# The last up unit of each feed-forward by halves of tokens

## The reference

```python
def swiglu(h, w_gu, w_down):
    gu = h @ w_gu
    g, u = jnp.split(gu, 2, axis=-1)
    return (jax.nn.silu(g) * u) @ w_down
```

## Time and profile before

| | |
|---|---|
| median of three runs | 2002.74 us (2000.58 to 2003.66) |
| span of the profiled execution | 1994.7 us |
| what lies around the span, against the median | 8.0 us |
| TensorE busy | 1939.8 us, 97% |
| VectorE busy | 1178.0 us, 59% |
| ScalarE busy | 977.8 us, 49% |

### The profile page before, as it was taken

One profiled execution on the slowest core, in us unless ns is written; L12 is line 12 of the kernel. 1 busy time (PEld: TensorE's weight loads), 2 busy tenths in 40 slices (PEclk: granted clock), 3 DMA queues, 4 the chain that ended last, 5 costly groups with the idle time before them and its releaser, 6 DMA issues.

```text
span 1994.7 us, 23044 instructions
## 1 busy us (share of the span) xinstructions
PE 1939.8 (97%) x8950; PEld 1559.6 (78%) x8950; DVE 1178.0 (59%) x1544; ACT 977.8 (49%) x1522; POOL 202.7 (10%) x273
## 2 busy tenths in 40 slices
PE   5999999999999999999999999999999999999998
PEld 4768768888888888668788888887777778888886
DVE  6777699899999999663443333335445453333323
ACT  4533268888888888553243222124455542222221
POOL 3200211131211110020010000001011110000001
PEclk9999999999999999999999999999999999999999
DMA  8564589999999999942322323223212142323201
GB/s 297 173 214 170 180 295 364 369 376 374 374 372 371 358 369 362 350 128 81 106 82 89 104 85 105 95 74 105 67 43 85 43 136 86 106 86 105 95 32 42
DMA packets 200024, 366.49 MB, mean 184 GB/s; under 512 B 13514, under 2 KB 84055, under 8 KB 199914
## 3 DMA queue, kind: packets, MB, share of 16 engines
q1 hardware_dynamic: 181152, 343.20, 49.1%
q10 hardware_dynamic: 8714, 11.17, 1.6%
q0 software_dynamic: 10048, 10.62, 1.6%
HBM read 365.05 MB, written 24.65 MB: 195 GB/s over the span
## 4 chain that ended last, share of the span: by engine, by line
PE 83%; DVE 7%; DMA 4%; ACT 2%; issue 2%; POOL 1%; ACTq 0%; POOLq 0%; DVEq 0%
PE ps L288 80%; DVE wlo L235 3%; DMA raw<-in_w_expert_gate 3%; ACT whi L216 1%; PE ps L2215 1%; DMA VR<-in_b_subln 1%; PE ps L2242 1%; DVE XT0l L2298 0%; PE ps L2907 0%; ACT YB L2307 0%; ACT whi L220 0%; DVE acc L285 0%; PE ps L790 0%; DVE hT4l L856 0%; DMA raw<-in_ada_w 0%
## 5 line engine op out<-in xcount | busy, mean ns | idle before, releaser
L235 DVE TENSOR_TENSOR wlo<-raw,whi 128x1024 fp32r<-128x1024 f32 x574 | 671.1, 1214 | 295.0 <-ACT whi L216 292.3
L216 ACT ACTIVATE whi<-raw 128x1024 fp32r<-128x1024 f32 x574 | 571.5, 1048 | 214.2 <-PE ps L288 191.1
L288 PE MATMUL ps<-hT5h,whi 128*128 128x512 f32 x352 | 137.0, 389 | 0.6 <-DVE hT5l L285 0.6
L288 PE MATMUL ps<-hT3h,whi 128*128 128x512 f32 x352 | 137.0, 389 | 0.6 <-DVE hT3l L285 0.6
L288 PE MATMUL ps<-hT5l,whi 128*128 128x512 f32 x352 | 136.9, 389 | 0.0
L288 PE MATMUL ps<-hT3h,wlo 128*128 128x512 f32 x352 | 136.9, 389 | 0.0
L288 PE MATMUL ps<-hT5h,wlo 128*128 128x512 f32 x352 | 136.9, 389 | 0.0
L288 PE MATMUL ps<-hT3l,whi 128*128 128x512 f32 x352 | 136.9, 389 | 0.0
L2770 DVE TENSOR_TENSOR tmpT<-tmpT,ps 128x512 f32<-128x512 f32 x44 | 30.1, 684 | 139.3 <-PE ps L288 139.3
L288 PE MATMUL ps<-whi,XT1h 128*128 128x512 f32 x256 | 102.7, 401 | 1.5 <-DVE XT1l L2298 1.5
L288 PE MATMUL ps<-whi,XT0h 128*128 128x512 f32 x256 | 102.7, 401 | 1.1 <-DVE XT0l L2298 1.1
(11 more groups left out here) (475 smaller groups left out, 4102.4 us busy)
## 6 DMA issues: line engine op xcount, KB each, us to landing
raw<-in_w_expert_gate SPq DMA_DIRECT2D x64, 1024.0 KB
raw<-in_w_expert_up SPq DMA_DIRECT2D x64, 1024.0 KB
raw<-in_w_expert_down SPq DMA_DIRECT2D x64, 1024.0 KB
raw<-in_ffn_w_gu SPq DMA_DIRECT2D x44, 1024.0 KB
raw<-in_ffn_w_down SPq DMA_DIRECT2D x20, 1024.0 KB
raw<-in_ada_w SPq DMA_DIRECT2D x24, 512.0 KB, 5.0
raw<-in_a_w_in SPq DMA_DIRECT2D x8, 1024.0 KB
raw<-in_kv_w SPq DMA_DIRECT2D x8, 1024.0 KB
```

Source lines behind the costliest of these rows:

```text
L216: e.activation(hi[:, c], raw[:, c], ACT.Copy).then_inc(self.S("w_hi"), 1)
L235: e.tensor_tensor(lo[:, c], raw[:, c], hi[:, c].bitcast(F32), ALU.subtract).then_inc(self.S("w_lo"), 1)
L288: return e.matmul(o, l, r, start=start, stop=stop, skip_group_check=True)
```

## The change

The last u unit of each feed-forward (`ng == 10`) is made by a new function. It goes through the tokens by halves: 256 moving columns into a bank of its own for each half and block, so four banks and 96 products in place of two banks and 48. VectorE multiplies and ScalarE and VectorE split the rows by the same halves. The low parts of this unit are so counted four times, and `a_lo` goes to 24 per feed-forward. The first half of the last down product waits at `tb == 0` for the rows of the first half of tokens and at `tb == 2` for those of the second half. Some semaphores are put together (`mix_lo` and `gm_lo` as `left_lo`, `mix_hi` and `gm_hi` as `left_hi`, `fga` and `fgb` as `final_in`), with the later waits moved on by the earlier counts.

```diff
-                    R.plan(f"fu{l}.{ng}", 2, V_)
-                    W.ends[W.index[f"fu{l}"][ng]] = R.full(f"fu{l}.{ng}", 1)
+                    R.plan(f"fu{l}.{ng}", 4 if ng == 10 else 2, V_)
+                    W.ends[W.index[f"fu{l}"][ng]] = R.full(f"fu{l}.{ng}", 3 if ng == 10 else 1)
...
+        def halves_pe(e, j, name, hT):
+
+            w = W.parts(j)
+            for half in range(2):
+                ts = slice(half * 256, half * 256 + 256)
+                for k in range(2):
+                    b = R.claim(e, name, 2 * half + k)
+                    for kc in range(KC):
+                        if half == k == 0 and kc % 4 == 0:
+                            e.wait_ge(*W.half(j, kc // 4))
+                        i = mm3(e, b[:, ts], [x[:, kc, k * P:(k + 1) * P] for x in w], [x[:, kc, ts] for x in hT], kc == 0, kc == KC - 1)
+                    i.then_inc(*R.fill(name, 2 * half + k))
+
+        def n_pe(e, js, name, hT, k_first, nk, chunk, later=None):
...
+                        if tb == 2 and later is not None:
+                            later(k0 + k)
...
+                        if ng == 10 and m == "fu":
+                            halves_pe(e, W.index[f"{m}{l}"][ng], f"{m}{l}.{ng}", hT)
+                            continue
...
-                             (lambda kc: e.wait_ge(S("a_lo"), 22 * l + f0 + kc + 1)) if h == 0 else None)
+                             (lambda kc: e.wait_ge(S("a_lo"), 24 * l + f0 + kc + 1)) if h == 0 else None,
+                             (lambda kc: e.wait_ge(S("a_lo"), 24 * l + f0 + kc + 3) if kc >= 4 else None) if nd == 8 else None)
...
-                    for k in range(2):
-                        e.wait_ge(*R.done(f"fu{l}.{ng}", k))
-                        if f == 0 and f0 > 0 and k == 0:
-                            e.wait_ge(*R.full(f"fd{l}.{f0 - 8}.1", 3))
-                        e.activation(AT[0][:, f + k, :], tmpT[k][:, :], ACT.Copy).then_inc(S("a_hi"), 1)
+                    for half in range(2 if ng == 10 else 1):
+                        ts = slice(256 * half, 256 * half + 256) if ng == 10 else slice(0, T)
+                        for k in range(2):
+                            e.wait_ge(*R.done(f"fu{l}.{ng}", 2 * half + k))
+                            if f == 0 and f0 > 0 and k == 0:
+                                e.wait_ge(*R.full(f"fd{l}.{f0 - 8}.1", 3))
+                            e.activation(AT[0][:, f + k, ts], tmpT[k][:, ts], ACT.Copy).then_inc(S("a_hi"), 1)
...
+                            e.tensor_tensor(tmpT[k][:, ts], tmpT[k][:, ts], R.bank(f"fu{l}.{ng}", i)[:, ts], ALU.mult).then_inc(
+                                *R.free(f"fu{l}.{ng}", i))
+                            e.wait_ge(S("a_hi"), 24 * l + f0 + f + 2 * half + k + 1)
+                            e.tensor_tensor(AT[1][:, f + k, ts], tmpT[k][:, ts], AT[0][:, f + k, ts].bitcast(F32),
+                                            ALU.subtract).then_inc(S("a_lo"), 1)
...
-                     (lambda kc: e.wait_ge(S("gm_lo"), kc + 1)) if h == 0 else None)
+                     (lambda kc: e.wait_ge(S("left_lo"), 8 + kc + 1)) if h == 0 else None)
```

More of the change, by code:

```diff
@@ L917, in t_pe @@
                     i.then_inc(*R.fill(*name[k]))
-        def n_pe(e, js, name, hT, k_first, nk, chunk):
+        def halves_pe(e, j, name, hT):
[10 more added lines that the diff above has]
+        def n_pe(e, js, name, hT, k_first, nk, chunk, later=None):
             bs = [None] * TB
@@ L1231, in mix_out_pe @@
                     if tb == 0:
-                        e.wait_ge(S("mix_lo"), kc - 3 if kc >= 4 else kc + 5)
+                        e.wait_ge(S("left_lo"), kc - 3 if kc >= 4 else kc + 5)
                     i = mm3(e, b[:, :], [x[:, kc, tb * P:(tb + 1) * P] for x in hT1], [x[:, kc % 4, :] for x in W.parts(j)],
@@ L1552, in first_act @@
                 e.wait_ge(*R.done("pw", gi))
-                e.activation(hT1[0][:, 4 + gi, :], PT[:, gi, 16:528], ACT.Copy).then_inc(S("mix_hi"), 1)
+                e.activation(hT1[0][:, 4 + gi, :], PT[:, gi, 16:528], ACT.Copy).then_inc(S("left_hi"), 1)
             ada_row_act(e, 3)
@@ L1566, in mix_high @@
                 e.wait_ge(S("hh"), h + 1)
-                e.activation(hT1[0][:, h, :], UC[h], ACT.Copy).then_inc(S("mix_hi"), 1)
+                e.activation(hT1[0][:, h, :], UC[h], ACT.Copy).then_inc(S("left_hi"), 1)
             squares(0)
@@ L1763, in mix_low @@
             def mix_low(c, x, k):
-                e.wait_ge(S("mix_hi"), k)
-                e.tensor_tensor(hT1[1][:, c, :], x, hT1[0][:, c, :].bitcast(F32), ALU.subtract).then_inc(S("mix_lo"), 1)
+                e.wait_ge(S("left_hi"), k)
+                e.tensor_tensor(hT1[1][:, c, :], x, hT1[0][:, c, :].bitcast(F32), ALU.subtract).then_inc(S("left_lo"), 1)
             def scaled(h):
@@ L2524, in join_vec @@
                 if tb == 0:
-                    e.wait_ge(S("fga"), 16)
+                    e.wait_ge(S("final_in"), 16)
                 e.tensor_tensor(XN[:, tb, :], X[:, tb, :], FGa[:, :], ALU.mult).then_inc(S("xn"), 1)
@@ L2669, in gmlp_act @@
                 e.wait_ge(S("gm"), gi + 1)
-                e.activation(hT2[0][:, gi, :], UT[:, gi, :], ACT.Copy).then_inc(S("gm_hi"), 1)
+                e.activation(hT2[0][:, gi, :], UT[:, gi, :], ACT.Copy).then_inc(S("left_hi"), 1)
             for j in W.index["go"]:
@@ L2704, in gmlp_vec @@
             for gi in range(8):
-                e.wait_ge(S("gm_hi"), gi + 1)
-                e.tensor_tensor(hT2[1][:, gi, :], UT[:, gi, :], hT2[0][:, gi, :].bitcast(F32), ALU.subtract).then_inc(S("gm_lo"), 1)
+                e.wait_ge(S("left_hi"), 8 + gi + 1)
+                e.tensor_tensor(hT2[1][:, gi, :], UT[:, gi, :], hT2[0][:, gi, :].bitcast(F32), ALU.subtract).then_inc(S("left_lo"), 1)
             for h in range(2):
@@ L2743, in ffn_act @@
                         if f0 + f > 0:
-                            e.wait_ge(S("a_lo"), 22 * l + f0 + f - 1 + k)
+                            e.wait_ge(S("a_lo"), 24 * l + f0 + f - 1 + k)
                         e.activation(tmpT[k][:, :], R.bank(f"fg{l}.{ng}", k)[:, :], ACT.Silu).then_inc(*R.free(f"fg{l}.{ng}", k))
@@ L2766, in ffn_vec @@
                         W.low(e, j + W.depth(j))
[L2767 to L2774, removed]
+                    for half in range(2 if ng == 10 else 1):
+                        ts = slice(256 * half, 256 * half + 256) if ng == 10 else slice(0, T)
+                        for k in range(2):
+                            e.wait_ge(*R.done(f"fg{l}.{ng}", k))
+                            i = 2 * half + k
+                            e.wait_ge(*R.full(f"fu{l}.{ng}", i))
+                            e.tensor_tensor(tmpT[k][:, ts], tmpT[k][:, ts], R.bank(f"fu{l}.{ng}", i)[:, ts], ALU.mult).then_inc(
[3 more added lines that the diff above has]
+                                            ALU.subtract).then_inc(S("a_lo"), 1)
                     ng += 1
@@ L3345, in _ @@
             pairs_sync(e, lambda tb: S(f"y_in{tb}"))
-            e.dma_start(FGa[:, :], g["final_g"].partition_broadcast(P)).then_inc(S("fga"), 16)
+            e.dma_start(FGa[:, :], g["final_g"].partition_broadcast(P)).then_inc(S("final_in"), 16)
             W.load(e, more_at + 4)
@@ L3373, in _ @@
             e.wait_ge(*R.done("as7", 7))
-            e.dma_start(GF[:, :], g["final_norm_2"].partition_broadcast(P)).then_inc(S("fgb"), 16)
+            e.dma_start(GF[:, :], g["final_norm_2"].partition_broadcast(P)).then_inc(S("final_in"), 16)
             ffn_act(e, own, 1, hT5, AT5, 4, 6, lambda tb: (f"ao0.{tb}",), lambda tb: (f"ao1.{tb}",))
@@ L3405, in last @@
                 if tb == 0:
-                    e.wait_ge(S("fgb"), 16)
+                    e.wait_ge(S("final_in"), 32)
                 if tb < TB - 1:
```

## The result

The changed kernel takes 2005.49 us (median of 20 runs, 2001.38 to 2011.65) against 2001.24 us before (20 runs, 1995.78 to 2005.67). The ratio is 1.0025, 95% interval [1.0016, 1.0034]: 5.0 us slower, between 3.2 and 6.8 (the two medians by themselves differ by 4.3). Forecast were 5.2 us more, and so 2008.0 on a base of 2002.74.

A forecast was written before the change was run, and what follows sets the result against it. The prediction took TensorE, 97% busy, to bound the kernel. Its terms, 2.6 us for the banks, 1.3 for products and 1.3 for the clock, gave 5.2 us over 2002.74, so 2008.0 us, range 2004.9 to 2011.2.

The forecast's parts named there:

- What bounds, and no stall behind the unit: Feed-forwards: TensorE, 97% busy, bounds; down products don't wait for the last u unit's rows, so finishing them earlier is worth 0.
- the 7 us of slack: Last down product: the last remainder is ready 7.2 us before the first product with chunk 4 needs it.
- VectorE and ScalarE: Last u unit's row steps, per feed-forward: VectorE works 0.7 us more, ScalarE 0.4, covered by idle time.
- TensorE's products: Last u unit: 96 products of 256 columns at 120.2 ns for 48 of 512: +0.65 us each, +1.3 for both.
- The banks: Attention's start: ring moved by two, so vv0.0 waits for VectorE's seventh remainder, 3.59 us late, part given back: +2.6 us.
- The clock: Pause of 4.0 us ahead of vv0.0: granted clock falls from 2.4 to 1.2 GHz, +1.3 us (0.7 to 1.8).
- The sum: Whole kernel: 2.6 + 1.3 + 1.3 = 5.2 us more, so 2008.0 us on a base of 2002.74.
- (a): At the pause ahead of vv0.0 the clock stays up: 3.9 us more, 2006.6 us; chance 0.13.
- (b): Last u unit: 256-column products cost half of 512-column ones: 3.9 us more, 2006.6 us; chance 0.20.
- (c): Last u unit: weight loads don't quite hide, 135 ns or more a product: 8.0 us more, 2010.7 us; chance 0.10.
- (d): Attention's start: the bank's wait isn't there or is taken up later, only products count: +1.3, 2004.0 us; chance 0.05.
- (e): Down products do wait for the last rows, ready 2.4 us sooner each: -4.8 us, 1997.9 us; chance 0.02.

The follow-up runs named there:

- experiment 6: Kernel before with chunks 4 and 5 first in the last down product's first half, 1.0036; same order on the changed kernel with attention's banks renumbered by two, 1.0004.
- experiment 5: Kernel before with all 22 u units made of 256-column products, into the same two banks: 1.0084 of before.
- experiment 4: Changed kernel with TensorE products filling the pause ahead of vv0.0: six calls 1.0047 of before, four calls 1.0010.
- Experiments 1 to 3: First two: changed kernel with attention's banks renumbered by two, 1.0021 and 1.0005 of before; third: kernel before with banks renumbered by minus two, 1.0029.
- the second comparison: Changed kernel timed again, beside itself with attention's banks renumbered by two, on one chip: 1.0036 of before against 1.0005.
- experiments 1 and 3: Changed kernel with attention's banks renumbered by two, 1.0021 of before; kernel before with them renumbered by minus two, 1.0029.
- experiment 1: Changed kernel with attention's fixed banks renumbered by two, so vv0.0 again takes the bank of feature 0: 1.0021 of before.

## Why the prediction was right

**What bounds, and no stall behind the unit.** Right. The added time of a feed-forward is that of its added products, 0.65 us, and experiment 6 showed what the 7 us of slack were worth by taking them away.

**VectorE and ScalarE.** Right. A quarter's step takes 0.41 to 0.43 us, where the estimates were 0.43 and 0.42. The rows come 2.1 us sooner, not 2.4, mainly since the last multiply starts only 0.27 us after the first down product (1340.98 against 1340.71), which the estimate of 1.3 us left out; nothing hangs on it.

**TensorE's products.** Right: 120 ns a product, +0.65 us a unit, in the profile and eleven units at a time in experiment 5. One thing under it was read wrongly: what I took for a plain fp32 product is one of two records that such a product leaves (experiment 4). The argument held, because it needs only the records: they follow each other at 112 ns, and the trace has a weight load for each of them (16 in that stretch).

**The banks.** Right in place, releaser and size: 4.33 us from the first low part's begin to vv0.0's start against a forecast of 4.42, and +2.55 us of attention with the clock held, forecast +2.6. The start is 3.50 us later than before, and 0.95 of it came back where the pause ahead of vv0.2 was. Experiments 1 to 3 showed the wait in both directions.

**The clock.** Right that it falls, too small in size: 1.3 us was taken, with 1.8 as the upper end, and it is 2.4. What was mis-sized is the length of the slow time. I took the one fall that the trace of before showed, 3.4 us, and let part of it lie in the pause; here it lasted 6.8 us (1380.1 to 1387.0), of which TensorE worked 5.1, and half of that is the price. The trace before had no long pause in mid-kernel from which to read it.

**The sum.** The terms give 2.6 + 1.3 + 1.3 = 5.2 where the stages show 2.55 + 1.3 + 2.4 = 6.25. The times, 5.0 us in [3.2, 6.8] and 1.0036 [1.0023, 1.0049] in the second comparison, hold both. That they came out within 0.2 us of the forecast is in part luck: the clock's term was 1.1 us short, and the measured 5.0 is itself 1.2 under the stages. The interval also holds 1.0020, so by the times alone it is open whether the change is over the 0.2% that the prediction asked about; the stages, 6.2 us or 0.31%, say that it is. The base needs a correction too: I put 8.0 us around the span; the changed kernel's profiled execution took 2001.38 us at a span of 1999.5, so only 1.9 us lie around it, and the rest will have been the difference between the profiled execution of before and the median. It did not matter for the difference, but the three runs of the base were 1.5 us above the median of twenty. With the same difference on 2001.24 the forecast would have been 2006.4, and the measured 2005.49 lies only 0.6 us inside the stated range.

**The rivals.** The clock that holds (a), products at half price (b), loads that don't hide (c), a wait that is taken up (d) and rows that are waited for (e) are each excluded by a run: the windows of the changed kernel, experiment 5 for two of them, experiments 1 and 3, and experiment 6.

## What to carry to other kernels

Count every resource that is handed out in turn, not only the instructions: two more banks in one unit moved all later claims, and where a part with fixed banks takes over from the ring, its first claim fell on a bank whose reader came seventh of eight. Before splitting a step to shorten a wait, look for the product that needs it first; the gain is the wait that is there, here none, and the price here was 13.5 to 13.8 ns for every product more. A pause costs more than its length when the clock falls in it: here 2.6 us for the wait and 2.4 for the products that ran at half clock behind it. Where runs scatter by more than the change is worth, compare the lengths of stages in profiles and use the times for the whole.

## What the runs showed of the hardware

- A fall of the clock to 1.2 GHz lasted 6.8 us in all three profiles with the pause of 3.4 to 3.9 us ahead of vv0.0 (one of them at a clock of 0.65 around it). With products in all of that pause but its first 0.3 us the clock stayed at 1.00 (the two profiles of experiment 4).
- Behind the last pauses of the attention, 0.7 and 1.6 us, it fell for 3.4 us in seven of the eleven profiles at full clock, and not in the other four. In experiment 1 that fall cost 0.4 us, since the slower products covered a wait of 1.0 us behind them.
- A product of 256 columns in fp32r with its own 128x128 load starts 120 ns after the one before, at 512 columns 226.8: 13.3 and 13.5 ns above the columns at 2.4 GHz, where a record of plain fp32 at 512 columns, 430 ns after the one before, has 3 above two clocks a column.
- Plain fp32 products leave two records each: six calls, twelve records, 0.43 us from start to start at 512 columns, so 0.86 us a product.
